# A new order of the sixteen attention groups, three gate buffers, and side tiles that may pass one another

## The reference, cut to what matters

```python
h = rms_norm(x, g_pre); proj = h @ w_in        # q k v z_a | conv: cb cc cx z_c | merge gates ga gc
s = (q @ k.T) * 64**-0.5 - slopes[h] * dist    # 4 heads, two maps each, causal
p = softmax(s); a = p[map 0] - lam * p[map 1]; o = a @ v
o = rms_norm(o, subln_gain) * (1 - lam_init)
y_attn = (o * silu(z_a)) @ w_attn_o            # z_a: the gate of the attention branch
y_conv = (cb * conv3(cc * cx) * silu(z_c)) @ w_conv_o
y = sigmoid(ga + b_a) * y_attn + sigmoid(gc + b_c) * y_conv
return x + rms_norm(y @ w_out, g_post)
```

## Time and profile before

| | us |
|---|---|
| median of 3 runs | 780.42 (778.79 to 782.7) |
| the profiled execution | 780.28 |
| its span, slowest core (core 4) | 778.7 |
| spans of the eight cores | 772.3 to 778.7 |
| PE busy in the span | 724.1 (93%) |
| DVE, ACT, POOL busy | 368.8, 377.5, 152.5 |
| attention stage, 165 to 545 us: PE busy of 380 | 348.1 |

### The profile page before, as it was taken

How to read it: one execution, slowest core, us unless ns; L and a number is a source line. 1 busy time by engine, 2 the same in 40 slices (tenths; PEclk the granted TensorE clock), 3 DMA queues, 4 the chain that set the end, 5 groups by cost and what they waited for, 6 DMA issues and landing times.

```text
span 778.7 us, 15293 instructions; the slowest of 8 cores (772.3 to 778.7 us)
## 1 busy us (share of the span) xinstructions
PE 724.1 (93%) x5370; PEld 382.2 (49%) x5370; DVE 368.8 (47%) x829; ACT 377.5 (48%) x552; POOL 152.5 (20%) x165
## 2 busy tenths in 40 slices
PE   4799999998888998799999999899999999999995
PEld 1354444455555454455555556555444444444442
DVE  3666444222654456657565467746522222222444
ACT  2446555264565654376666667675222222223433
POOL 1100000105711000010100001101333332321663
PEclk9999999998999999899999999999999999999998
DMA  7997973810000110000100101002852222200786
GB/s 166 246 209 203 252 168 68 128 22 2 2 2 29 28 18 12 2 15 15 29 2 2 28 2 28 3 1 56 134 123 41 41 42 40 42 1 1 247 293 221
DMA packets 39684, 57.68 MB, mean 74 GB/s; under 512 B 23825, under 2 KB 24209, under 8 KB 39346
## 3 DMA queue, kind: packets, MB, share of 16 engines
q1 hardware_dynamic: 31682, 39.58, 18.4%
q0 software_dynamic: 7776, 16.78, 13.8%
q10 hardware_dynamic: 144, 0.26, 0.1%
HBM read 59.76 MB, written 8.39 MB: 88 GB/s over the span
## 4 chain that ended last, share of the span: by engine, by line
PE 84%; DVE 7%; issue 4%; ACT 2%; DMA 1%; DVEq 0%; POOL 0%; SPq 0%; ACTq 0%; POOLq 0%
PE psum L1428 14%; PE psum L823 13%; PE psum L1159 12%; PE psum L725 11%; PE psum L711 8%; PE psum L1481 7%; PE psum L1435 7%; PE psum L1099 6%; PE psum L858 4%; ACT arena L1128 2%; DVE arena L1199 1%; PE psum L688 1%; DVE arena L1204 1%; PE psum L1239 1%; DMA arena<-gpre 1%
## 5 line engine op out<-in xcount | busy, mean ns | idle before, releaser
L1128 ACT ACTIVATE arena<-psum 128x1024 bf16<-128x1024 f32 (+2 forms) x259 | 219.0, 902 | 112.5 <-PE psum L1099 111.9
L1159 PE MATMUL psum<-arena 128*128 128x130 bf16 x1780 | 134.0, 223 | 5.3 <-DVE arena L1199 2.8
L1159 PEld LDWEIGHTS psum<-arena 128*128 128x128 bf16 x1780 | 106.0, 99 | 54.2 <-issue 47.9
L823 PE MATMUL psum<-arena 128*128 128x512 bf16 x512 | 126.3, 389 | 5.7 <-DVE arena L1186 2.1
L1428 PE MATMUL psum<-arena 128*128 128x512 bf16 x512 | 115.7, 379 | 0.0
L1440 ACT ACTIVATE arena<-psum,arena 128x512 f32<-128x512 f32 x64 | 44.0, 687 | 120.4 <-PE psum L1428 120.4
L1444 DVE SCALAR_TENSOR_TENSOR arena<-arena,psum 128x512 f32<-128x512 f32 x64 | 43.8, 687 | 115.8 <-PE psum L1435 115.8
L725 PE MATMUL psum<-arena 128*128 128x512 bf16 x384 | 88.4, 379 | 0.0
L1099 PE MATMUL psum<-arena 64*128 64x512 bf16 (+3 forms) x568 | 73.8, 340 | 6.3 <-ACT arena L1128 3.9
L1428 PEld LDWEIGHTS psum<-arena 128*128 128x128 bf16 x512 | 50.1, 98 | 60.2
L823 PEld LDWEIGHTS psum<-arena 128*128 128x128 bf16 x512 | 47.6, 99 | 54.9 <-issue 12.6
(11 more groups left out here) (101 smaller groups left out, 626.3 us busy)
## 6 DMA issues: line engine op xcount, KB each, us to landing
arena<-x_perm SPq DMA_DIRECT2D x48, 512.0 KB, 6.4
arena<-w_chunk POOLq DMA_DIRECT2D x40, 256.0 KB, 4.8
out_own<-arena SPq DMA_DIRECT2D x15, 512.0 KB, 4.7
arena<-w_y POOLq DMA_DIRECT2D x8, 256.0 KB, 5.5
arena<-wo_r POOLq DMA_DIRECT2D x1, 2048.0 KB, 20.6
arena<-w_wide POOLq DMA_DIRECT2D x4, 256.0 KB, 11.4
arena<-w_wide POOLq DMA_DIRECT2D x1, 1024.0 KB, 11.9
arena<-gpost SPq DMA_DIRECT2D x1, 512.0 KB, 3.6
```

The costliest lines, as they stand in the source:

```text
L823: p.op("pe", (lambda e: e.matmul(bank(bk), lhsT=lhs(kc), rhs=rhs(kc), start=(kc == 0), stop=(kc == n - 1))), reads=rd, writes=[("bank", bk)])
L1128: p.op("act", (lambda e, a0=a0, a1=a1, c0=c0, c1=c1, bias=bias: e.activation(out=PT[sl][:, a0:a1, c0 * 128:c1 * 128], in_=psum[:, a0:a1, c ...
L1159: p.op("pe", (lambda e, kd=kd, m=m, cb=cb, acc=acc, first=first, vj=vj: e.matmul(acc, lhsT=PT[sl][:, 2 * kd + m, cb * 128:(cb + 1) * 128], ...
```

## The change

The sum of the work on every engine stays what it is. What changes:

- **Order.** Behind the branch the groups are now (2,2) (3,0) (2,3) (0,0) (3,1) (0,1) (1,2) (2,0) (2,1) (1,0) (1,3) (1,1). The four ahead of the branch stay.
- **Three sz buffers** instead of two, and the z tile of a group is pushed at the group's first unit without waiting for anything.
- **Passing.** A transposition now names the four gated blocks that it reads (`need`). If by the planner's clock they are not there yet when a tile is to be started, `next_ready` lets the first tile of another kind go first.
- The planner's condition for the norm pieces asks for the piece that used the buffer, instead of counting, and the list of finished norms may be filled in any order.

```diff
-            sz = [reg(sz_off + i * 2 * K, 2 * K, F32).rearrange("p (b n) -> p b n", b=4) for i in range(2)]
...
+            NZ = 3
+            sz_at = [sz_off, sz_off + 2 * K, take(2 * K)]
+            sz = [reg(a, 2 * K, F32).rearrange("p (b n) -> p b n", b=4) for a in sz_at]
...
             def z_tile(s, h, g):
-                tb = g % 2
+                tb = g % NZ
...
-                while pieces and not kq_left and pieces[0][0] < 2 + len(normed) and p.now["pool"] < until:
+                while pieces and not kq_left and (pieces[0][0] < 2 or pieces[0][0] - 2 in normed) and p.now["pool"] < until:
...
-                    if i == len(NORMS) - 1:
+                    if len(normed) == len(NORMS):
...
-            GROUPS = [(s, h) for one, two in ((3, 0), (2, 1)) for h in HEADS for s in (one, two)]
+            GROUPS = [(3, 2), (0, 2), (3, 3), (0, 3)]
+
+            GROUPS += [(2, 2), (3, 0), (2, 3), (0, 0), (3, 1), (0, 1), (1, 2), (2, 0), (2, 1), (1, 0), (1, 3), (1, 1)]
...
-                                                                  in1=sz[ob][:, qb, :], op0=ALU.mult, op1=ALU.mult)),
-                         reads=[("oraw", ob, qb), ("rs", ob), ("sz", ob)], writes=[("gat", ob, qb)], t=0.345)
+                                                                  in1=sz[g % NZ][:, qb, :], op0=ALU.mult, op1=ALU.mult)),
+                         reads=[("oraw", ob, qb), ("rs", ob), ("sz", g % NZ)], writes=[("gat", ob, qb)], t=0.345)
...
-                    tile_ = {"mm": mm, "post": post, "n": 4, "w": 0.057}
+                    tile_ = {"mm": mm, "post": post, "n": 4, "w": 0.057, "need": [("gat", ob, qb) for qb in range(4)]}
...
-                    side.append((g, 0.35, lambda qb=qb: gate(qb), [("rs", ob), ("sz", ob), ("z", g)]))
+                    side.append((g, 0.35, lambda qb=qb: gate(qb), [("rs", ob), ("sz", g % NZ), ("z", g)]))
...
+            def next_ready():
+
+                if p.when(fill.q[0].get("need", [])) > now["pe"] + 0.1:
+                    later = [k for k, t in enumerate(fill.q) if "need" not in t]
+                    if later:
+                        fill.q.insert(0, fill.q.pop(later[0]))
+
...
                     if fill.left() <= TAIL:
                         break
+                    if not fill.open:
+                        next_ready()
                     one()
...
                     if g:
-                        z_wait = (s, h, g)
+                        fill.push(z_tile(s, h, g))
                     late -= 0.057 * 4 * KC + 0.057 * 4
                 if last:
                     drain(g - 2)
-                if z_wait and not any(x[0] <= g - 2 for x in side):
-                    fill.push(z_tile(*z_wait))
-                    z_wait = None
```

More of the change, by code:

```diff
@@ L485, in emission @@
                 p.place(("zr", i), zr_off[i], 2 * K)
-                p.place(("sz", i), sz_off + i * 2 * K, 2 * K)
             p.place(("wz",), wz_off, 8 * K)
@@ L491, in emission @@
             p.place(("tz",), tz_off, 2 * K)
+            for i in range(NZ):
+                p.place(("sz", i), sz_at[i], 2 * K)
             for i in range(NR):
```

## The result

| | before | after |
|---|---|---|
| median, us | 780.42 | 769.55 (768.57 to 770.28) |
| ratio, 95% interval | | 0.9882 [0.9858, 0.9906] |
| profiled execution, us | 780.28 | 770.28 |
| spans of the eight cores, us | 772.3 to 778.7 | 763.4 to 768.7 |

The ratio compares runs of both kernels that were taken side by side; 0.9882 x 780.42 is 771.2 us. Executions in a slower state of the chip (one of the kernel before, 809.36 us) are left out of all times and ratios here. Two parts of the page of after, busy times and the 40 slices, answer to the earlier trace rows. PE's row holds 5290 matmuls of 5370; the records of 80 are missing in that core's trace, so its PE time is too low and waits appear where nothing stood. I therefore read core 6, whose records are complete.

What follows compares the result with a forecast made beforehand. PE was taken as the bound, busy 724.1 of 778.7 us, so only its idle time and clock could move. Terms -7.40 - 3.85 + 2.04 + 1.1 - 1.0 = -9.1 from 780.3 gave 771.2 us, range 767.9 to 774.8.

Steps and rivals of the forecast that it cites:

- The two stops: In short groups (3,0) and (0,0), waits of a transposition and convolution tile behind a z tile go: -7.40 us.
- The slow rows: PE rows at the lowered clock behind the long waits in (3,0) and (0,0) return to ordinary times: -3.85 us.
- the stops only move: Rival: power, gates, transposition end as late in (2,2) and (2,3), the long waits return there; 779 to 782 us, chance 0.10.
- The pairs: Convolution tiles directly behind a transposition: three more places where PE stops 0.68 us, +2.04 us.
- the releasers that were named: Sign: six stops of about 0.68 us ahead of L826, released by the transposition's reader (L1251) or epilogue's first step (L1191).
- Close z tiles: Side tiles close behind a z tile, eight instead of five: +1.1 us, ends 0.45 and 1.8.
- the waits for L875: Sign: PE's waits for the z tile's reader should add up to less than 2 us.
- Parting (2,0) and (1,0): Separating these two short groups halves PE's stops in and at the end of (1,0): -1.0 us, ends 0 and -2.1.
- Ahead of the branch: Groups ahead of the branch, including the slow z tile behind group 2: counted 0, with -1.5 us as an end.
- DVE as the limit of the short groups: Rival: DVE has nothing to spare in (3,0) and (0,0), which keep 3.1 us of idle time; 776.3 us, chance 0.17.
- The slower case: Rival: the clock falls at new short stops behind transpositions and z tiles, about 1.8 us each; 783 to 790 us, chance 0.07.
- the row of the prediction: Trace row at 400 to 410 us: a 0.68 us stop behind a transposition leaves the granted clock at 1.00.

Runs made afterwards that it cites:

- The run without pairs: Changed kernel with filling paused behind each filled-in transposition, so no convolution tile directly follows it: stretch 299.1 us against 302.4, ratio 0.9855.
- the run with the old end of the list: Changed kernel with the last five groups as of old, (1,3) (2,0) (1,0) (2,1) (1,1): stretch 300.9 us against 302.4, ratio 0.9875.
- the late reading: Changed kernel with the branch's flag read directly ahead of the branch, some 40 us later: stretch 299.0 us, ratio 0.9833.
- the run with more work on DVE: Changed kernel with four unused 128x128 products on DVE behind the transpositions of eight groups: stretch 302.4 us, ratio 0.9894.

## Why the prediction was right, point by point

The forecast of 771.2 us and the measured ratio agree, and -9.1 us stand against -9.4 in the stretch. The sum is right; its terms are less so. PE's waits ahead of rows fell from 22.8 to 19.2 us in the mean of the six cores of each kernel whose records are complete, 3.6 us where the forecast had 5.3 (-7.40 + 2.04 + 1.1 - 1.0). The rows themselves took 5.8 us less where it had 3.85. What follows compares core 7 of before with core 6 of after; on these two the waits fell by 3.4 and the rows by 5.6 us.

- **The two stops, -7.40.** They went, in full. The reason given was half wrong. The z tile pushed early, "what the third buffer allows", does nothing by itself: with the old order the transpositions wait for the gate's product, up to 3.56 us, and the kernel is no faster. The other half of the sentence, a full group ahead of each short one, is what carries it, and even this was too strict: one full group among the three is enough. Nor did PE stand still 7.40 us less: other waits took half of it, and in the run with the new order alone nearly all of it. The rival "the stops only move" had the mechanism right, and it is what the old order with three buffers does; where a full group stands among the three it does not apply.
- **The slow rows, -3.85.** Gone; the clock is 1.00 from 245 us on. In addition the slow z tile behind group 2 went, with the row ahead of it some 1.6 us on core 7, which I had counted at 0 with -1.5 as an end; before, it was slow on six of the eight cores, behind three short stops of which the changed kernel has only one (last section). Three transpositions that took 1.00 us in step with the gate now take 0.38, -1.9 us, and their waits of 1.4 us went too. The forecast had no term for it. Without passing both are back, but in the run with the new order alone PE never waits for the gate either, so no single part of the change does this.
- **The pairs, +2.04.** 2.0 to 4.1 us, six of 0.68, with the releasers that were named. The run without pairs gives 3.3 us back. At five of them the clock stays at 1.00. The sixth stands behind the flag, where the clock had fallen already, and did not cause the fall: in the kernel without pairs the rows at this place are as slow, on core 0 1.03 and 1.90 us for rows that take 0.61 and 1.08 at full clock.
- **Close z tiles, +1.1.** Right: eight places with 2.9 us against five with 1.7, +1.2. But the waits for L875, which I had named as under 2 us in all, are these and so make 2.9; my own term had said as much.
- **Not in the forecast.** Convolution tiles behind other convolution tiles, +0.9, most of it the two stops of 0.83 us for ACT. The scores' waits +0.5, other small ones +0.6.
- **Parting (2,0) and (1,0), -1.0.** The term that failed: it brought nothing, as the run with the old end of the list shows. The waits of L1164 for `epilogue`, two of which I had meant to halve, were 2.7 us and are 2.9.
- **Ahead of the branch, 0.** The fall of the clock behind the flag grew: the rows there lost some 1.6 us to it before and 2.5 after, +0.9. On cores 3 and 7 they lose only about 1.3 after, which is the spread of 301.5 to 302.8 us between the cores. Both kernels with two buffers, before and the new order alone, show the one size on all cores; those with three buffers that read the flag early show two. Why stays open; that the wait for the flag is behind the fall at all, the late reading shows.

Put together: the waits, -7.4 + 2.0 + 1.2 - 1.4 + 0.9 + 0.5 + 0.6, make -3.6, and 3.4 was measured on these two cores. The rows, -3.85 - 1.6 - 1.9 + 0.9, make about -6.4 where 5.6 was measured; 0.8 us of that I can't place. Gains that I had left out made up for the term that brought nothing and the waits that I had not seen, so that the direction and the two stops were foreseen, while the agreement of the sum to a tenth of a microsecond is luck. One reading ahead of the sum was off too, without weight in it: ACT and DVE, 377.5 and 368.8 us, are busy a little more than half as long as PE's 724.1, not less.

**The other rivals.** DVE as the limit of the short groups falls by the idle time left in them, 1.34 us together; the run with more work on DVE does not test it. The slower case falls too, since in the changed kernel the clock fell at none of the pairs and behind none of the eight z tiles, on any core. At these places the row of the prediction held against the section "A second HAM failure mode: psum-queue depth-cycling" of the Trainium skill's "TensorE: Matmul & The Clock Gate". The traces don't refute that section: in other kernels here the clock did fall on some cores behind stops of under 1 us, as the last section shows.

## What to carry to other kernels

When an engine waits behind a buffer, ask what the producer behind that buffer waits for: one more buffer only shows the next wait, while interleaving long and short work gives the late path time to end. Look at the granted clock together with the idle time: the new order alone left PE's idle time as it was and still gained 7.2 us, since its rows ran at full clock. Read a computed flag where it is needed and not where it becomes ready, since a read that waits stops the engine's whole queue. Compare variants by a stretch that all of them share and that the change touches; here it agreed to 0.2 us between the cores of the kernel before, when whole spans differed by 6.

## What the runs showed of the hardware

The same stop lowers the clock on some cores and not on others of one execution. In the kernel with (3,0) first behind the branch, the transposition waits 1.42 us and the convolution tile 0.68 on all eight cores. Core 1, and then core 6:

```profile
296.10 0.38 PE L1244 MATMUL psum<-arena 128*128 128x128 bf16 x4 [1.42 <-DVE arena L987]
297.16 1.89 PE L826 MATMUL psum<-arena 128*128 128x512 bf16 x8 [0.68 <-DVE arena L1191]
```
```profile
294.59 0.38 PE L1244 MATMUL psum<-arena 128*128 128x128 bf16 x4 [1.42 <-DVE arena L987]
295.65 3.49 PE L826 MATMUL psum<-arena 128*128 128x512 bf16 x8 [0.68 <-DVE arena L1191]
```

The convolution tile takes 1.89 us on cores 1 to 4 and 3.28 to 3.49 on cores 0, 5, 6 and 7. The same cores part some 60 us earlier, the other way round: behind the flag, the convolution tile runs at full clock, 1.89 us, on cores 0, 5, 6 and 7, and slowly on 1 to 4 (2.9 us for eight matmuls on cores 1 and 3). So cores on which the clock came back sooner behind the flag reached the next stop 1.0 to 1.2 us earlier, and there the clock fell again. What in that time decides was not settled. Behind the longer stops of 2.63 and 3.56 us in the two kernels with the old order the rows were slow on all eight cores, and behind the one of 2.47 us in the kernel before on six.

A fall of the clock was also seen behind stops of under 1 us, where several stand close together. In the kernel that reads the flag late, group 2 ends with three stops, 0.15, 0.48 and 0.21 us. Core 2, and then the z tile on core 4, behind stops of 0.15, 0.48 and 0.20:

```profile
265.14 0.55 PE L957 MATMUL psum<-arena 128*128 128x32 bf16 x16 [0.15 <-DVE arena L1019]
...
266.98 0.39 PE L1164 MATMUL psum<-arena 128*128 128x130 bf16 x4 [0.48 <-DVE arena L1204]
267.58 0.85 PE L1164 MATMUL psum<-arena 128*128 128x130 bf16 x8 [0.21 <-DVE arena L1209]
268.43 3.49 PE L861 MATMUL psum<-arena 128*128 128x128 bf16 x32
```
```profile
270.36 1.95 PE L861 MATMUL psum<-arena 128*128 128x128 bf16 x32
```

The z tile behind them is slow on two cores there, on two with the new order alone, and on six in the kernel before, where the same three stops stand ahead of it. In the changed kernel only a stop of 0.21 us stands ahead of it, and it takes 1.95 us on all eight cores. Whether the stops alone decide it is not shown: on the other cores the same three leave the clock up.
